# A hybrid decoder layer with 32 experts: routing and first dispatch in another order, and each pair's dispatch inside the pair before

## Chip, cores and metric

One Trainium2 chip, one of its cores. The metric is the time of one execution on the device in microseconds (us), median of the runs.

## What is computed

A decoder layer in float32 over 256 tokens of 1024 channels. First a mixer (differential attention, a pooling branch, attention into a memory, gates, output projection) gives `h`. Then a sparse layer of 32 experts, in which each token goes to its four best:

```python
logits = rmsnorm(h, g_ffn) @ w_router + b_router       # 256 x 32
top_val, top_idx = lax.top_k(logits, 4); gates = softmax(top_val)
# for every expert e, over the tokens that chose it:
g = minimum(xb @ w_gate[e] + b_gate[e], 7.0)
u = clip(xb @ w_up[e] + b_up[e], -7.0, 7.0)
out = (g * sigmoid(1.702 * g) * (u + 1.0)) @ w_down[e] + b_down[e]
y = y.at[rows].add(out * gates)                         # result: h + y
```

Each expert's three matrices are 1024 x 1024, 12.6 MB together, 403 MB for all.

## The kernel before

The code writes the program of every engine by hand: each engine runs its own list in order, with semaphores between them. There is no planner.

**The mixer** runs in 48 units of 128 tokens by 512 columns. A unit is the work of `unit_k` (line 1331 holds the products, three for each of 8 blocks), in one of three banks of PSUM. Units 44 to 47 are the output projection: columns 0 to 511 of tile 0 and of tile 1, then the other columns of both. `add_h` (L1137) adds each to the residual X, which gives h.

**Routing.** `turn_h` transposes h in four pieces (L1295), `copy_hT` (L1143) copies them with the gain to HNT, `logits` (L1541) multiplies by the router's weights. ScalarE sums the squares of h (`h_square`, L789), GpSimd (POOL) makes the inverse root of the mean (L483, L485, `inverse_root`). On VectorE `route` (L1160 to L1174) scales the logits, takes the four best and writes MASK; `weigh` (L1181 to L1184) makes the gates; `norm_h` (L1151) writes the normalised rows HN. When both tiles have a mask, TensorE multiplies them by a triangular matrix and by ones (L1561). That gives each token's rank in each expert and each expert's number of tokens, from which VectorE computes the number of rounds (each has room for SLOTS = 64 tokens per expert; here one round is enough). L1565 transposes the gates; L1570 reads the number of rounds into a register of TensorE.

**The experts** run in 16 pairs. `build_slots` compares iota with the ranks: PT (L1227), 128 tokens by 2 x 64 slots in 0 and 1, and PW (L1224), the same times the gates. At the start of a pair TensorE dispatches (L1612): HN by PT gives the gathered rows XE, transposed, in banks 4 and 5, which ScalarE (L808) and VectorE (L1255) copy. L1617 transposes PW. Then `project` (L1592, with the biases at L1598 and L1599) for gate and up of the first expert, `combine` (L1580) adds the pair before into the tokens, `project` for the second expert, and for each expert the transposes of its activations AH (L1295), a copy by ScalarE (L819) and the product with w_down (L1644), copied by L822 and L1280. `slots_free` says that PW is transposed; then VectorE builds the slots of the next pair and BIAS_PICK (L1259), before it reads bank 0 (L1263, signal `g_read`).

**The weights.** Each pair needs twelve loads of 2 MB, in the order gate, gate, up, up of the first expert, the same of the second, then w_down twice for each. They go to nine slots of 16 KB a partition (`experts_ring`). SP issues them in order (L415); a load waits until the slot's last load has been used (semaphore `used`, once for each load). Eighteen loads of a turn of 24 run over the nine slots twice, the last six take only six of them:

```python
MOE_SLOT = (8, 5, 4, 6, 0, 2, 1, 3, 7)
TURN_SLOT = [MOE_SLOT[q % RING] for q in range(2 * RING)] + [MOE_SLOT[q] for q in range(1, 7)]
```

So in the second pair, load 27 (counted from 0) takes the slot of load 20, load 28 that of 21. The first nine loads are issued while the mixer ends, gated by its units; the last of these waits for both logits.

## Time and profile before

| | |
|---|---|
| time, median of 3 runs | 1244.7 us (1244.56 to 1244.71) |
| the profiled execution | 1244.2 us, its span 1242.2 us |
| mean granted clock of TensorE | 0.996 |
| TensorE busy | 1166.5 us (94%), weight loads 578.7 us |
| VectorE, ScalarE, GpSimd busy | 440.4, 259.1, 49.3 us |
| moved by DMA | 458.51 MB, mean 369 GB/s |
| chain that ended last | PE 75%, DMA 17%, DVE 4%, ACT 2%, issue 2% |

PE is TensorE, DVE VectorE, ACT ScalarE, POOL GpSimd, SP the engine that issues the loads. L with a number is a line of the kernel. The page cuts the span into 40 slices. The chain that ended last is followed back from the last instruction, at each step to what released it. A pair of numbers at the start of a row is start and duration in us. Matmuls in float32 are run in two passes, so a count (x32) is twice the number of products in the code; passes are pipelined, and the mean of one overlaps the next.

### The profile page before, as it was taken

To read this page: it belongs to the slowest core of one execution; us is meant where nothing else is said; L and a number is where in the kernel's file an instruction comes from. 1 tells how busy PE (TensorE), PEld (TensorE's weight loads), DVE (VectorE), ACT (ScalarE), POOL (GpSimd) and SP (SyncE) were. 2 spreads that over 40 slices of the span, in tenths; PEclk is the share of its full clock that TensorE was granted. 3 is DMA by queue.
4 is the path that set the end of the run, shared out by engine and by line. 5 is a ranking of instruction groups with operands and counts; after the bars stand their busy time and mean duration, and the time that the engine had idled before them with its cause. 6 is when DMAs were issued, how large, how long until landed. Compare 5 with 4: busy or idle time off the path is not lost.

```text
span 1242.2 us, 13980 instructions
## 1 busy us (share of the span) xinstructions
PE 1166.5 (94%) x5428; PEld 578.7 (47%) x5428; DVE 440.4 (35%) x775; ACT 259.1 (21%) x414; POOL 49.3 (4%) x72
## 2 busy tenths in 40 slices
PE   8999999998899999999999999999999999999897
PEld 5887888877434434343434344343434332433332
DVE  4878798765412121212122122212122121212122
ACT  5555477531100100010001001000100010010100
POOL 2222101101000000000000000000000000000000
PEclk9999999999899999999999999999999999999999
DMA  9455545597799999999999999999999999999996
GB/s 361 153 195 169 194 147 202 185 348 304 309 425 394 394 430 429 428 428 429 429 428 428 428 430 428 427 428 429 429 428 427 429 429 428 427 429 429 428 428 271
DMA packets 54825, 458.51 MB, mean 369 GB/s; under 512 B 4304, under 2 KB 5200, under 8 KB 30224
## 3 DMA queue, kind: packets, MB, share of 16 engines
q1 hardware_dynamic: 53408, 454.15, 88.4%
q0 software_dynamic: 1104, 3.93, 0.9%
q8 instruction: 15, 0.25, 0.1%
q10 hardware_dynamic: 288, 0.10, 0.0%
q14 instruction: 10, 0.08, 0.0%
HBM read 457.11 MB, written 1.05 MB: 369 GB/s over the span
## 4 chain that ended last, share of the span: by engine, by line
PE 75%; DMA 17%; DVE 4%; ACT 2%; issue 2%; POOL 0%; SPq 0%; POOLq 0%; DVEq 0%
PE bank L1592 30%; PE bank L1331 15%; DMA experts_ring<-in_w_down 15%; PE bank L1644 14%; PE bank L1612 5%; PE bank L1580 4%; PE bank L1598 2%; DMA ring<-in_w_mem_kv 1%; ACT region L819 1%; PE bank L1295 1%; PE bank L1599 1%; DMA ring<-in_w_out 1%; DVE ring_split L839 1%; DVE region L1246 1%; ACT region L822 1%
## 5 line engine op out<-in xcount | busy, mean ns | idle before, releaser
L1592 PE MATMUL bank<-experts_ring,region 128*64 128x512 f32 x2048 | 454.2, 596 | 11.5 <-DVE region L1255 6.5
L1592 PEld LDWEIGHTS bank<-experts_ring,region 128*64 128x64 f32 x2048 | 145.1, 137 | 291.9 <-issue 286.4
L1644 PE MATMUL bank<-experts_ring,region 128*64 128x512 f32 x1024 | 229.0, 596 | 32.0 <-ACT region L819 25.0
L1331 PE MATMUL bank<-ring_split,region_split 128*128 128x512 f32 x736 | 217.0, 396 | 0.5 <-DVE ring_split L850 0.3
L1644 PEld LDWEIGHTS bank<-experts_ring,region 128*64 128x64 f32 x1024 | 73.1, 137 | 167.3 <-issue 125.7
L1331 PEld LDWEIGHTS bank<-ring_split,region_split 128*128 128x128 f32 x736 | 136.0, 188 | 31.1 <-issue 2.3
L839 DVE TENSOR_TENSOR ring_split<-ring,ring_split 128x2048 fp32r<-128x2048 f32 x42 | 96.2, 2291 | 41.4 <-ACT ring_split L588 41.1
L1331 PE MATMUL bank<-ring_split 128*128 128x512 f32 x272 | 106.4, 391 | 0.0
L1280 DVE COPY region<-bank 64x512 f32<-64x512 f32 x32 | 22.2, 693 | 237.3 <-PE bank L1644 237.3
L1263 DVE TENSOR_SCALAR region<-bank 128x512 f32<-128x512 f32 x32 | 22.1, 692 | 209.7 <-PE bank L1599 209.7
L588 ACT ACTIVATE ring_split<-ring 128x2048 fp32r<-128x2048 f32 x42 | 80.3, 1912 | 30.8 <-DMA ring<-in_w_in 10.0
L1270 DVE TENSOR_SCALAR region<-bank 128x512 f32<-128x512 f32 x32 | 22.1, 692 | 180.0 <-PE bank L1599 180.0
L812 ACT ACTIVATE region<-region 128x512 f32<-128x512 f32 x32 | 20.2, 630 | 287.6 <-DVE region L1263 287.6
L1580 PE MATMUL bank<-region 128*128 128x512 f32 x136 | 65.7, 606 | 13.4 <-DVE region L1246 12.4
L822 ACT ACTIVATE region<-bank 64x512 f32<-64x512 f32 x32 | 18.9, 590 | 242.1 <-PE bank L1644 242.1
L1612 PEld LDWEIGHTS bank<-region 128*128 128x128 f32 x512 | 60.1, 197 | 15.3 <-issue 12.2
L1612 PE MATMUL bank<-region 128*128 128x128 f32 x512 | 63.1, 283 | 2.6 <-DVE region L1224 2.6
L1331 PEld LDWEIGHTS bank<-ring_split 128*128 128x128 f32 x272 | 51.1, 188 | 11.1
L1246 DVE TENSOR_TENSOR region<-bank,region 128x512 f32<-128x512 f32 x68 | 45.4, 687 | 14.3 <-PE bank L1580 14.3
L1580 PEld LDWEIGHTS bank<-region 128*128 128x128 f32 x136 | 24.2, 189 | 46.2 <-DVE region L1246 31.7
L1295 PE MATMUL bank<-con,region 128*128 128x128 f32 x240 | 37.0, 286 | 7.0 <-DMA con<-in_table 4.6
L816 ACT ACTIVATE region<-bank 128x256 f32<-128x256 f32 x16 | 6.1, 383 | 173.3 <-PE bank L1580 173.3
(163 smaller groups left out, 677.4 us busy)
## 6 DMA issues: line engine op xcount, KB each, us to landing
experts_ring<-in_w_gate SPq DMA_DIRECT2D x64, 2048.0 KB, 26.1
experts_ring<-in_w_up SPq DMA_DIRECT2D x64, 2048.0 KB, 25.2
experts_ring<-in_w_down SPq DMA_DIRECT2D x64, 2048.0 KB, 28.0
ring<-in_w_in SPq DMA_DIRECT2D x28, 1024.0 KB, 5.2
ring<-in_w_mem_kv SPq DMA_DIRECT2D x4, 1024.0 KB, 11.4
ring<-in_w_b_attn SPq DMA_DIRECT2D x4, 1024.0 KB, 6.3
ring<-in_w_out SPq DMA_DIRECT2D x4, 1024.0 KB, 8.7
region<-in_b_gates POOLq DMA_DIRECT2D x6, 512.0 KB, 4.5
```

Of the source, the lines that this page charges most:

```text
L588: nc.scalar.activation(upper(H), raw(H), ACT.Copy).then_inc(hi_act, 1)
L822: nc.scalar.activation(OE[e * SLOTS:(e + 1) * SLOTS, 0:HALF], bank[2][0:SLOTS, :], ACT.Copy).then_inc(o_lo, 1)
L839: nc.vector.tensor_tensor(lower(H), raw(H), upper(H), ALU.subtract).then_inc(lo_ready, 1)
L1246: nc.vector.tensor_tensor(X[:, t, h * HALF:(h + 1) * HALF], bank[6 + j % 2][:, :], X[:, t, h * HALF:(h + 1) * HALF], ALU.add).then_inc(y_a ...
L1280: nc.vector.tensor_copy(OE[e * SLOTS:(e + 1) * SLOTS, HALF:D], bank[2][SLOTS:2 * SLOTS, :]).then_inc(o_hi, 1)
L1295: ins = nc.tensor.transpose(dst[:, b * P:(b + 1) * P], srcs[b], ident)
L1331: ins = nc.tensor.matmul(UB[u % 3][:, :], a[:, k, toks], b[:, cols], start=(k == 0 and m == 0), stop=(k == k_n - 1 and m == 2))
L1580: nc.tensor.matmul(bank[6 + j % 2][:, :], PWT[:, t * P:(t + 1) * P], OE[:, h * HALF:(h + 1) * HALF], start=True, stop=True).then_inc(comb_ ...
L1592: ins = nc.tensor.matmul(dst[h * SLOTS:(h + 1) * SLOTS, :], XE[:, kk, e * SLOTS:(e + 1) * SLOTS], w[:, k, h * HALF:(h + 1) * HALF], start= ...
L1598: nc.tensor.matmul(dst[:, :], pick, BIAS_UP, start=False, stop=False)
L1612: ins = nc.tensor.matmul(bank[4 + half][:, b * P:(b + 1) * P], HN[:, t, 4 * half + b, :], PT[:, t, :], start=(t == 0), stop=(t == NT - 1))
L1644: ins = nc.tensor.matmul(bank[2][h * SLOTS:(h + 1) * SLOTS, :], AHT[:, k, half * SLOTS:(half + 1) * SLOTS], w[:, k, h * HALF:(h + 1) * HAL ...
```

## The change

- TensorE's order around units 46 and 47: tile 0's first transposes stand inside unit 46, two more inside unit 47, tile 0's logits and half of tile 1's before the last three blocks of unit 47. Tile 0's rank products come right after unit 47, its dispatch after tile 1's logits; tile 1 adds its part to both. Tile 1's logits go to bank 0.
- `norm_h` is gone. `gain_h` writes HN as h times the gain, in four halves; the inverse root is multiplied into PT instead. `route` has one operation less, and the last square covers half of tile 1's row, since the other half's is taken earlier (POOL adds the two).
- iota counts from 1, so that the ranks need no subtraction.
- The first pair's dispatch and the copies of XE stand before the loop. In the loop the dispatch of the next pair stands behind the transposes of the first expert's activations, also in the last pair. PW's transposes stand behind the first `project`.
- HN moves to another buffer and keeps its columns in order; w_gate and w_up are laid out to match on the host, by `projection_rows`.

```diff
-    c[:, C_IOTA:C_IOTA + P] = np.tile(np.arange(SLOTS), 2)[None, :]
+    c[:, C_IOTA:C_IOTA + P] = np.tile(np.arange(SLOTS) + 1, 2)[None, :]
...
+def projection_rows(w):
+    w = np.asarray(w)
+    return np.ascontiguousarray(w.reshape(EXPERTS, KD, P, D).transpose(0, 2, 1, 3).reshape(EXPERTS, D, D))
...
 # gpsimd
-            for t in range(NT):
-                pool.wait_ge(squares, 5 + t)
-                inverse_root(stat[:, 4 + t:5 + t], EPS, h_inv)
+            pool.wait_ge(squares, 6)
+            inverse_root(stat[:, 4:5], EPS, h_inv)
+            pool.wait_ge(squares, 7)
+            inverse_root(stat[:, 5:6], EPS, h_inv, stat[:, 6:7])
...
 # scalar
+            def xe_lower_half(n):
+                act.wait_ge(disp_done, n * 2 + 1)
+                nc.scalar.activation(XE[:, 0:4, :], bank[4][:, :].rearrange("p (k n) -> p k n", k=4),
+                                     ACT.Copy).then_inc(xe_lo, 1)
+            h_square(0, X[:, 1, 0:HALF], 5, 2)
+            h_square(1, X[:, 0, :], 4, 3)
+            logit_exp(0)
+            h_square(2, X[:, 1, HALF:D], 6, 4)
+            logit_exp(1)
+            xe_lower_half(0)
...
-                        act.wait_ge(disp_done, it * 2 + 1)
-                        nc.scalar.activation(XE[:, 0:4, :], bank[4][:, :].rearrange("p (k n) -> p k n", k=4),
-                                             ACT.Copy).then_inc(xe_lo, 1)
...
                             nc.scalar.activation(AHT, bank[3][:, :].rearrange("p (j s) -> p j s", j=4),
                                                  ACT.Copy).then_inc(actT_copied, 1)
+                            if e == 0:
+                                xe_lower_half(it + 1)
...
 # vector
-            def norm_h(t):
+            def gain_h(t, h):
+                cols = slice(h * HALF, (h + 1) * HALF)
                 dve.wait_ge(late_in, 32)
...
+                nc.vector.tensor_tensor(HN[:, t, cols], X[:, t, cols], GFF[:, cols], ALU.mult).then_inc(hn_ready, 1)
...
-                nc.vector.memset(zero, 0.0)
...
+                link(nc.vector.tensor_tensor_scan(run, equal, no_logits, count, ALU.add, ALU.add))
+                link(nc.vector.scalar_tensor_tensor(out=equal, in0=run, scalar=float(TOP_K), in1=equal, op0=ALU.is_le, op1=ALU.mult))
...
+            add_h(44)
+            gain_h(0, 0)
+            add_h(45)
+            copy_hT(0, 0, 0)
+            gain_h(1, 0)
+            add_h(46)
+            copy_hT(1, 1, 0)
+            copy_hT(2, 0, 1)
+            gain_h(0, 1)
             route(0)
             weigh(0)
             add_h(47)
...
+            def expert_slots(first, t):
+                for e in range(2):
+                    cols = slice(e * SLOTS, (e + 1) * SLOTS)
+                    nc.vector.tensor_scalar(PT[:, t, cols], iota[:, cols], RANKS[:, t, bass.ds(first + e, 1)],
+                                            stat[:, 4 + t:5 + t], ALU.is_equal, ALU.mult).then_inc(slots_built, 1)
...
+            dve.wait_ge(first_rank_done, 1)
+            dve.wait_ge(mask_ready, 1)
+            first_slots(0, bank[3][:, 0:32])
             copy_hT(3, 1, 1)
-            norm_h(0)
             route(1)
-            weigh(1)
-            norm_h(1)
-            dve.wait_ge(gate_ready, 2)
+            gain_h(1, 1)
             dve.wait_ge(rank_done, 1)
+            dve.wait_ge(mask_ready, 2)
+            first_slots(1, bank[3][:, 32:64])
...
+            weigh(1)
+            dve.wait_ge(gate_ready, 2)
+            xe_upper_half(0)
+            expert_weights(0)
+            next_round_pair(slice(0, NT))
...
-                        dve.wait_ge(disp_done, it * 2 + 2)
-                        nc.vector.tensor_copy(XE[:, 4:8, :], bank[5][:, :].rearrange("p (k n) -> p k n", k=4)).then_inc(xe_hi, 1)
-                        dve.wait_ge(slots_free, it + 1)
-                        build_slots(i * 2 + 2)
...
+                        dve.wait_ge(slots_free, it + 1)
+                        for t in range(NT):
+                            expert_slots(i * 2 + 2, t)
+                        expert_weights(i * 2 + 2)
...
+                        xe_upper_half(it + 1)
...
 # tensor
-            unit(46)
...
+            unit_k(46, 0, 4)
+            pe.wait_ge(h_ready, 1)
+            turn_h(0, 0, 0)
+            unit_k(46, 4, KD)
             unit_k(47, 0, 2)
+            pe.wait_ge(h_ready, 3)
+            turn_h(1, 1, 0)
+            turn_h(2, 0, 1)
+            unit_k(47, 2, 5)
             pe.wait_ge(hT_copied, 3)
             pe.wait_ge(late_in, 32)
-            logits(0)
-            unit_k(47, 2, KD)
+            logits(0, 0, KD)
+            logits(1, 0, 4)
+            unit_k(47, 5, KD)
+            pe.wait_ge(mask_ready, 1)
+            nc.tensor.matmul(bank[3][:, 0:32], tri, MASK[:, 0, :], start=True, stop=True)
...
             pe.wait_ge(h_ready, 4)
             turn_h(3, 1, 1)
             pe.wait_ge(hT_copied, 4)
-            logits(1)
+            logits(1, 4, KD)
+            pe.wait_ge(slots_built, 2)
+            pe.wait_ge(hn_ready, 3)
+            dispatch_tile(0)
             pe.wait_ge(mask_ready, 2)
...
+            pe.wait_ge(slots_built, 4)
+            pe.wait_ge(hn_ready, 4)
+            dispatch_tile(1)
             pe.wait_ge(gate_ready, 2)
...
-                        pe.wait_ge(slots_built, it * 8 + 4)
-                        for half in range(2):
-                            for b in range(4):
-                                for t in range(NT):
-                                    ins = nc.tensor.matmul(bank[4 + half][:, b * P:(b + 1) * P], HN[:, t, 4 * half + b, :], PT[:, t, :],
-                                                           start=(t == 0), stop=(t == NT - 1))
-                            ins.then_inc(disp_done, 1)
+                        pe.wait_ge(xe_lo, it + 1)
+                        pe.wait_ge(xe_hi, it + 1)
+                        project(it, turn, s, 0, 0, 0, bank[0])
                         pe.wait_ge(slots_built, it * 8 + 8)
                         for t in range(NT):
                             ins = nc.tensor.transpose(bank[3][:, t * P:(t + 1) * P], PW[:, t, :], ident)
                         ins.then_inc(slots_free, 1)
-                        pe.wait_ge(xe_lo, it + 1)
-                        pe.wait_ge(xe_hi, it + 1)
-                        project(it, turn, s, 0, 0, 0, bank[0])
                         project(it, turn, s, 0, 1, 2, bank[1])
...
                             turn4(bank[3], [AH[:, e, j * P:(j + 1) * P] for j in range(4)], actT_done)
+                            if e == 0:
+                                dispatch(it + 1)
```

`dispatch_tile(t)` is tile t's eight products of a dispatch, `dispatch(n)` waits for the slots of pair n and runs both tiles. `first_slots(t)` makes RANK from the rank products and builds tile t's two columns of PT; `expert_weights` builds PW as `build_slots` did; `xe_upper_half(n)` is VectorE's copy of bank 5.

## Rows read from the trace of the kernel before

**Rows 1.** The page's forty slices: TensorE's clock in tenths, bytes per second.

```profile
PEclk9999999999899999999999999999999999999999
...
GB/s 361 153 195 169 194 147 202 185 348 304 309 425 394 394 430 429 428 428 429 429 428 428 428 430 428 427 428 429 429 428 427 429 429 428 427 429 429 428 428 271
```

**Rows 2.** Table by stretches: length, busy by engine, granted clock, DMA share, GB/s.

```profile
308.00:318.20 10.20, 6.35 (x29) 5.88 (x30) 6.77 (x35) 1.79 (x3) 0.00 (x0) 0.50 0.99 423
320.00:326.00 6.00, 5.18 (x28) 1.87 (x28) 2.57 (x10) 0.29 (x1) 0.00 (x0) 1.00 0.01 3
326.00:380.00 54.00, 51.05 (x241) 19.98 (x239) 12.86 (x24) 4.60 (x8) 0.00 (x0) 1.00 1.00 415
380.00:427.00 47.00, 44.66 (x196) 15.87 (x194) 9.61 (x13) 3.42 (x6) 0.00 (x0) 1.00 0.95 383
427.00:1225.00 798.00, 749.93 (x3482) 292.25 (x3478) 179.88 (x336) 81.81 (x126) 0.00 (x0) 1.00 1.01 429
```

**Rows 3.** Timeline of TensorE, 287 to 337 us, with idle time before.

```profile
296.42 1.88 PE L1541 MATMUL bank<-region 128*128 128x32 f32 x16
...
303.26 0.66 PE L1295 MATMUL bank<-con,region 128*128 128x128 f32 x4 [0.79 <-DVE region L1137]
304.70 1.97 PE L1541 MATMUL bank<-region 128*128 128x32 f32 x16 [0.78 <-DVE region L1143]
309.22 2.34 PE L1561 MATMUL bank<-region,con 128*128 128x32 f32 x10 [2.55 <-DVE region L1174]
...
321.18 7.09 PE L1592 MATMUL bank<-experts_ring,region 128*64 128x512 f32 x32 [0.82 <-DVE region L1255]
```

**Rows 4.** The chain that ended last, 300 to 430 us: start, duration, what.

```profile
302.51 0.70 DVE region L1137
...
307.11 0.26 DVE region L1160
...
314.62 5.54 PE bank L1612 x32
...
373.21 3.77 PE bank L1612 x32
...
377.81 7.09 PE bank L1592 x32
...
413.55 0.60 ACT region L819
...
414.20 7.11 PE bank L1644 x32
...
422.76 7.09 PE bank L1644 x32
```

**Rows 5.** The loads' line, 417 to 419 us: load 27, issue and landing.

```profile
L415 SPq DMA_DIRECT2D experts_ring<-in_w_up x1: 333/333/333, 417.9 to 417.9; - x1
...
DMA to landing us min/median/max: 9.3/9.3/9.3
```

**Rows 6.** Timeline of POOL, 295 to 308 us: both inverse roots' powers.

```profile
296.07 0.58 POOL L485 TENSOR_TENSOR stat<-stat,small 128x1 f32<-128x1 f32 x1
...
304.78 2.30 POOL L485 TENSOR_TENSOR stat<-stat,small 128x1 f32<-128x1 f32 x1
```

**Rows 7.** The tile `rounds`: TensorE's load of the number of rounds, with its start.

```profile
L1570 PEldq TENSOR_LOAD <-rounds x1: 488/488/488, 313.3 to 313.3; - x1
```

**Rows 8.** The loads' line, 409 to 410 us: landing of load 25.

```profile
DMA to landing us min/median/max: 7.3/7.3/7.3
```

**Rows 9.** The loads' line, 412 to 414 us: landing of load 26.

```profile
DMA to landing us min/median/max: 9.2/9.2/9.2
```

**Rows 10.** Timeline of TensorE, 1214 to 1236 us: the last pair's w_down products.

```profile
1215.04 0.60 PE L1295 MATMUL bank<-con,region 128*128 128x128 f32 x4
...
1225.79 3.65 PE L1644 MATMUL bank<-experts_ring,region 128*64 128x512 f32 x16 [0.88 <-ACT region L819]
1230.43 3.65 PE L1644 MATMUL bank<-experts_ring,region 128*64 128x512 f32 x16 [0.99 <-DMA experts_ring<-in_w_down]
```

More of the change, by code:

```diff
@@ L1284, in _ @@
                 dve.wait_ge(rank_ready, r * 2 + 3)
-                next_round_pair()
+                next_round_pair(slice(0, NT))
                 dve.wait_ge(rank_ready, r * 2 + 4)
@@ L1533, in _, with logits @@
             unit(45)
-            unit(46)
             def turn_h(n, t, h):
                 turn4(bank[3 + n], [X[:, t, (4 * h + b) * P:(4 * h + b + 1) * P] for b in range(4)], hT_done)
-            def logits(t):
-                for k in range(KD):
-                    ins = nc.tensor.matmul(bank[7][:, t * EXPERTS:(t + 1) * EXPERTS], HNT[:, k, t * P:(t + 1) * P], WR[:, k, :],
+            def logits(t, first, after):
+                for k in range(first, after):
+                    ins = nc.tensor.matmul(bank[(7, 0)[t]][:, 0:EXPERTS], HNT[:, k, t * P:(t + 1) * P], WR[:, k, :],
@@ L1542, in logits, with dispatch_tile @@
                                            start=(k == 0), stop=(k == KD - 1))
-                ins.then_inc(logit_done, 1)
-            for n, (t, h) in enumerate(((0, 0), (1, 0), (0, 1))):
-                pe.wait_ge(h_ready, n + 1)
-                turn_h(n, t, h)
+                if after == KD:
+                    ins.then_inc(logit_done, 1)
+            def dispatch_tile(t):
+                for half in range(2):
+                    for b in range(4):
+                        ins = nc.tensor.matmul(bank[4 + half][:, b * P:(b + 1) * P], HN[:, t, (4 * half + b) * P:(4 * half + b + 1) * P],
+                                               PT[:, t, :], start=(t == 0 and b == 0), stop=(t == NT - 1), skip_group_check=True)
+                    if t == NT - 1:
+                        ins.then_inc(disp_done, 1)
```

100 lines of the change are left out of this document (48 added, 52 removed).

## Prediction

> **What bounds the kernel now.** I read the slices of the page first, to see which resource is full in which part. TensorE's clock is full nearly everywhere, and from the sixteenth slice on the bytes per second stand at 427 to 430 GB/s without a dip [rows 1]. The expert stage streams 192 loads of 2048 KB, which is 2.097 MB each; at 429 GB/s one takes 4.89 us and the twelve of a pair of experts 58.7 us. The table by stretches then shows where this stream is not full: nothing moves between 320 and 326 us, only 383 GB/s between 380 and 427, and 429 from there to 1225 [rows 2]. In the chain that ended last, a pair takes TensorE 56.63 us (321.18 to 377.81) [rows 3, 4]. So TensorE is 2 us a pair quicker than the stream: while it still has the ring of slots full, loads wait for slots that TensorE frees; once that lead is used up, only the stream counts. The end of the kernel is therefore the landing of the load that was last held up for a slot, plus 4.89 us for each load behind it, plus a tail. I count loads from 0. Every step of 4.89 us from load 27 on is of that unbroken kind, so load 27, issued at 417.9 and landed 9.3 us later [rows 5], fixes the rest. It takes the slot of load 20, the first w_down load of the second pair. Because SP issues in order and slots come back in the order of the turn, it waits for that load to be used.
>
> So a gain on the way to the first pair reaches the end only as far as it frees the slot of load 20 earlier. That is where I work it out: start of the first pair, length of that pair, place of load 20 in the next, landing, tail.
>
> **The start of the first pair.** Before, it is 321.18 [rows 3]. I walk the new order with the durations of the old one, at the full clock.
> - Unit 46 ends with four transposes inside it instead of behind, unit 47 with half of the second logits inside. The transposes are only moved. Half the logits is half of 1.88 us, 0.94 [rows 3]. Unit 47, which ended at 302.5 (the residual add that reads it starts at 302.51 [rows 4]), ends at 303.45. That delays the residual add, and SP's loads 6 and 7, by 0.95 us. Nobody needs those before 334 us.
> - The first tile's routing runs on VectorE from about 300.6, behind both its logits and the copy work, and takes 2.0 us; it ends before unit 47 and TensorE does not wait for it. Its three rank products, six of the logits' 0.12 us passes (0.7 us), fill the time in which TensorE waited for the residual add, which was 0.79 us idle [rows 3].
> - Add 303.5 to 304.2, transposes to 304.9, copy to 305.65 (0.7 each as before), half the logits 0.95 to 306.65. While TensorE transposes, VectorE builds the first tile's ranks and slots (0.25 and twice 0.25), which the copy just waits out.
> - Before, the second route waited for the inverse root: POOL's power took 2.30 us beside VectorE's long normalisation, against 0.58 alone [rows 6], and the route began at 307.11 [rows 4]. Now the last square is over half a row, the long normalisation is gone and the gains are applied elsewhere. So root ready at 306.3, route at 306.8. It ends at 308.75 with one operation less (2.1 us before, from 307.11 [rows 4] to the ranks at 309.22 [rows 3]).
> - TensorE does the first tile's dispatch (half of 3.77 us, 1.9 [rows 4]) from 306.65 to 308.6, covered by that route. Without that cover it would cost its 1.9 us. Then four rank passes (0.5) to 309.3; gain_h(1,1), 0.7 us, runs beside them and just covers them.
> - Ranks and slots of the second tile 0.8 us to 310.2, dispatch 1.9 to 312.1, copies of XE 0.7 to 312.8. The gate weights, the count of rounds and the weighted slots (2.7 us before the old dispatch) lie beside or behind this on VectorE. TensorE's transposes of the gates and its load of the round count follow the dispatch; from that load at 313.3 to the first work behind it at 314.62 were 1.3 us [rows 4, 7], the same as would give 313.4 to 313.7 here.
> By rows 313.8. A dozen hand-overs are each rounded to 0.05 us, and I take 314.2, bounds 313.7 and 315.5: **7.0 us earlier**. Part of it is the clock: the old stretch 308 to 318.2 ran at half of it (1.2 GHz) [rows 2], and the dispatch in it took 5.54 us instead of 3.77 [rows 4].
>
> **The pair.** The dispatch no longer stands between two pairs. From its start to the next project were 4.6 us (373.21 to 377.81, [rows 4]); what is left is a restart, for which no row stands (bounds 0 and 0.6, the issue gap there; I take 0.25). The two transposes of PW go behind the first projection and still cost about 0.4. The dispatch goes behind the transposes of AH, 3.77 us; it hides the wait for ScalarE's copy, 0.67 us (413.53 to 414.20 [rows 4]). Sum −4.6 + 0.25 + 0.4 + 3.77 − 0.67 = **−0.9 us a pair**. But load 20 is the first behind that dispatch: within its pair it is used 0.4 + 3.1 = **3.5 us later**. The slots of the next pair (1.7 us on VectorE) are now built only after PW's transposes, ahead of the read of bank 0. That delays g_read by about 2 us, but TensorE needs that bank only after the next projection and the combine, 8 us or more on, so nothing. BIAS_PICK is built at the start of the pair and first read 7 us on, the halves of XE are copied some 15 us before their first product: nothing either.
>
> **Landing.** Load 27 is issued 7.0 + 0.9 − 3.5 = 4.4 us earlier (bounds 2.9 and 4.9). The stream in front of it no longer reaches so far: loads 25 and 26 are issued over 7 us earlier and land by about 414, just when load 27 is issued. A load that found the stream nearly empty landed in 7.3 us [rows 8], against the 9.3 of load 27 [rows 5], but the one behind it lost about 1 us (load 26 took 9.2 [rows 9]). I give load 27's train 8.7 us, 0.6 better than before; bounds 0 and 1.4. The unbroken stream, and so the end of it at 1230.4, comes **5.0 us earlier**.
>
> **Tail.** In the last pair a dispatch is done too, for a pair that doesn't exist. Before, TensorE was still ahead of the stream: it took the third w_down load at 1225.79, was done with it 0.99 us too early for the last, and took that at 1230.43 [rows 10]. Now the first w_down product starts after a dispatch, at about 1219.3 in the old time, runs through two loads (7.1), and with the 8.56 us between the starts of two such products (414.20 to 422.76 [rows 4]) the last two begin at 1227.85 and end at 1234.95 instead of 1234.1: **+0.9**, bounds 0.6 and 1.4. All loads have the same size and the packets of w_gate and w_up stay as long; their new order costs the device nothing.
>
> Sum: −5.0 + 0.9 = **−4.1 us**. The profiled execution took 1244.2 (span 1242.2) and would take 1240.1; the median of the runs, 1244.7, becomes **1240.6**. In short, the change is the start of the first pair minus 318.3: every us of that start counts in full.
>
> **The rivals.**
> - The clock falls again. Before, it fell at 308.0 after TensorE had done only logits of 32 columns, 2.0 us of work in the 4.1 us before [rows 2, 3]. In the new order transposes and a dispatch stand in that place, which speaks against; waits remain between 303.5 and 306.7, which speaks for. The price is 1.8 us for a whole dispatch and about 0.1 us for each rank, logits or transpose pass, together 2 us: start at 316.2, time **1242.6**. The Trainium skill (TensorE: Matmul & The Clock Gate, The HAM clock gate) says that the throttled clock is the default and recent activity releases it; by that rule thinning out dense work, as here in front of the ranks, speaks for this rival.
> - The ring doesn't hold. If the queue in front of load 27 were still over 4 us long, the delay of 3.5 us inside the pair would not be felt, and the end would be earlier by 7.0 + 0.9 − 0.9 or so: **1237.7**. Against it: that load already had just enough queue before.
> - The stream is the bound anyway, and the some 13 us of gaps in it (6.0, 1.8 and 5.0 us by the bytes of three stretches [rows 2]) don't depend on TensorE's start (loads 6 to 8 even come 0.95 us later). Then only the tail is left: **1245.6**. Against it: the gap from 320 to 326 ends with the first used slot.
> - Slower: the mid-pair dispatch holds load 20's slot while the routing gives nothing back, because a half clock through the whole of it (44 passes more at 0.1 us) and a slow root (1.7 us) eat the 7.0. Start 321.2, 3.5 − 0.9 − 0.6 + 0.9 = +2.9: **1247.6**. It would be slower from a start at 320.8 on. No row shows both at once.
>
> **How the numbers follow.** A measurement of this kernel can tell about 0.2%, 2.5 us, from no change. Forecast 0.62, of its own 1239.2 to 1242.2 (start 313.7 to 315.5, the bounds of landing and tail half used); clock 0.18; ring free 0.07; stream alone 0.07; slower 0.06. Faster by over 2.5 us means under 1242.2: forecast and free ring, 0.69. Within: 0.25. Slower, 0.06. The range from 1238.6 to 1244.0 takes in the forecast and the clock, 0.80.
>
> **What would show it.** The first expert product starts near 314; no stretch of half clock, or one of few us; the power on POOL takes 0.6 us; the first pair lasts 55.7; load 27 is issued near 413.5 and lands 8 to 9 us later; no gap in the stream behind it; the last two loads are multiplied without a wait between them. It would be wrong if the start lies after 316, if another load than 27 is the last one held, or if TensorE's restart between the pairs is longer than 1 us.

## The result, and the profile after

The changed kernel takes **1238.55 us** (median of 5 runs, 1237.13 to 1239.02) against 1244.7 before: ratio 0.9947, 95% interval 0.9936 to 0.9959. That is 6.15 us less; 4.1 were forecast, and the time lies 0.05 us under the lower end of the range. The same kernel run again (after_again below) took 1237.43. The profiled execution took 1238.0 with a span of 1236.2 us.

The page's slices after: TensorE's clock in tenths and bytes per second. Against [rows 1] the slice of 8 tenths is gone, and the dip that followed the start of the loads takes one slice (297) instead of two (304 and 309).

```profile
PEclk9999999999999999999999999999999999999999
...
GB/s 360 153 199 170 189 153 204 177 342 297 412 388 429 397 429 428 428 428 428 428 429 428 429 428 429 428 429 428 429 427 429 428 429 428 430 427 430 427 430 253
```

The table by stretches after, to be read beside [rows 2] (stretch, length, busy time by engine, granted clock, DMA share, GB/s):

```profile
302.00:306.00 4.00, 3.02 (x23) 2.54 (x22) 2.59 (x8) 0.72 (x2) 0.87 (x2) 0.99 0.62 193
306.00:309.30 3.30, 3.30 (x17) 3.30 (x17) 2.35 (x10) 0.32 (x1) 0.00 (x0) 0.50 0.96 412
309.30:314.00 4.70, 2.84 (x24) 2.43 (x22) 3.24 (x17) 0.97 (x2) 0.00 (x0) 1.00 1.03 439
320.00:326.00 6.00, 6.00 (x30) 2.22 (x28) 3.11 (x10) 0.63 (x1) 0.00 (x0) 1.00 0.96 393
326.00:380.00 54.00, 52.36 (x250) 20.65 (x246) 12.63 (x24) 4.33 (x8) 0.00 (x0) 1.00 0.97 406
380.00:427.00 47.00, 45.34 (x216) 18.69 (x214) 10.71 (x15) 5.52 (x9) 0.00 (x0) 1.00 0.99 407
427.00:1218.00 791.00, 739.30 (x3444) 289.48 (x3442) 184.06 (x333) 70.34 (x115) 0.00 (x0) 1.00 1.01 428
```

The stretch from 320 to 326, which carried 3 GB/s before, now carries 393 GB/s; 380 to 427 rose from 383 to 407. The half clock (0.50, the lower of the two levels, 1.2 GHz) is left in one stretch of 3.3 us instead of 10.2.

TensorE's timeline after, from the ranks of the first tile to the first expert product (start, duration, what, idle time before it and who ended it), beside [rows 3]:

```profile
302.54 0.30 PE L1609 MATMUL bank<-region,con 128*128 128x32 f32 x2
...
303.49 0.66 PE L1331 MATMUL bank<-con,region 128*128 128x128 f32 x4 [0.20 <-DVE region L1155]
304.93 1.08 PE L1576 MATMUL bank<-region 128*128 128x32 f32 x8 [0.78 <-DVE region L1161]
305.84 3.66 PE L1584 MATMUL bank<-region 128*128 128x128 f32 x16
309.34 0.31 PE L1621 MATMUL bank<-region,con 128*128 128x32 f32 x2
...
310.72 2.05 PE L1584 MATMUL bank<-region 128*128 128x128 f32 x16 [0.85 <-DVE region L1226]
...
314.04 4.51 PE L1656 MATMUL bank<-experts_ring,region 128*64 128x512 f32 x20 [1.05 <-DVE region L1239]
```

The start of the first pair came from 321.18 to 314.04. The same 16 passes of a dispatch take 3.66 us in the half clock and 2.05 out of it.

The seams of the pair, first in the kernel before (last w_down products, dispatch, gate transposes, next projection; then transposes of AH and the w_down products), then after (transposes, dispatch, w_down; then last w_down and next projection):

```profile
366.12 7.09 PE L1644 MATMUL bank<-experts_ring,region 128*64 128x512 f32 x32 [0.87 <-ACT region L819]
373.14 3.84 PE L1612 MATMUL bank<-region 128*128 128x128 f32 x32
376.81 0.38 PE L1617 MATMUL bank<-con,region 128*128 128x128 f32 x2
377.81 7.09 PE L1592 MATMUL bank<-experts_ring,region 128*64 128x512 f32 x32 [0.61 <-issue]
...
412.92 0.60 PE L1295 MATMUL bank<-con,region 128*128 128x128 f32 x4
414.20 2.37 PE L1644 MATMUL bank<-experts_ring,region 128*64 128x512 f32 x10 [0.69 <-ACT region L819]
```

```profile
349.35 0.60 PE L1331 MATMUL bank<-con,region 128*128 128x128 f32 x4
349.78 3.74 PE L1584 MATMUL bank<-region 128*128 128x128 f32 x32
353.45 7.09 PE L1703 MATMUL bank<-experts_ring,region 128*64 128x512 f32 x32
...
361.99 7.09 PE L1703 MATMUL bank<-experts_ring,region 128*64 128x512 f32 x32 [0.87 <-ACT region L835]
368.91 3.61 PE L1656 MATMUL bank<-experts_ring,region 128*64 128x512 f32 x16
```

From the start of the last w_down products to the next projection: 11.69 us before (366.12 to 377.81), 6.92 after (361.99 to 368.91), 4.77 less. From the transposes of AH to w_down: 1.28 before (412.92 to 414.20), 4.10 after (349.35 to 353.45), 2.82 more. The first pair lasts 54.87 us instead of 56.63.

In the loads' own records load 27 is issued at 411.98 and lands 7.36 us later, load 28 is issued at 415.56 and lands 9.94 us later:

```profile
L423 SPq DMA_DIRECT2D experts_ring<-in_w_up x1: 333/333/333, 412.0 to 412.0; - x1
...
DMA to landing us min/median/max: 7.4/7.4/7.4
```

```profile
L423 SPq DMA_DIRECT2D experts_ring<-in_w_gate x1: 332/332/332, 415.6 to 415.6; - x1
...
DMA to landing us min/median/max: 9.9/9.9/9.9
```

A landing is reported in sixteen parts, and these times are those of the last part. By the last parts load 27 comes 5.63 us behind load 26 and load 28 comes 6.16 behind load 27; by the mean of the parts it is 6.03 and 4.99. Behind them the steps are 4.89 to 4.98 by the mean. POOL's power now takes 0.57 us, against the 2.30 of [rows 6]:

```profile
304.68 0.57 POOL L493 TENSOR_TENSOR stat<-stat,small 128x1 f32<-128x1 f32 x1
```

The last pair after, to be read beside [rows 10]: a dispatch for nobody, and then two w_down loads at a time without a wait between them.

```profile
1209.95 2.51 PE L1584 MATMUL bank<-region 128*128 128x128 f32 x21
1212.39 7.09 PE L1703 MATMUL bank<-experts_ring,region 128*64 128x512 f32 x32
1219.41 0.66 PE L1331 MATMUL bank<-con,region 128*128 128x128 f32 x4
1220.95 7.09 PE L1703 MATMUL bank<-experts_ring,region 128*64 128x512 f32 x32 [0.88 <-ACT region L835]
```

### The profile page after: what moved, and what is told of

Its sections match the earlier page's. It is cut to its first block, busy times and chain, and to the rows that moved or that the text cites. A ratio compares the mean times of both kernels' runs of the same rounds, so it can differ in the third digit from the quotient of the medians.

```text
span 1236.2 us, 14082 instructions
## 1 busy us (share of the span) xinstructions
PE 1165.1 (94%) x5460; PEld 581.9 (47%) x5460; DVE 446.3 (36%) x775; ACT 249.8 (20%) x409; POOL 47.8 (4%) x72
## 4 chain that ended last, share of the span: by engine, by line
PE 67%; DMA 28%; DVE 3%; ACT 1%; issue 1%; SPq 0%; POOL 0%; DVEq 0%; POOLq 0%
PE bank L1656 26%; DMA experts_ring<-in_w_up 26%; PE bank L1367 17%; PE bank L1703 8%; PE bank L1644 5%; PE bank L1584 4%; PE bank L1662 2%; PE bank L1331 1%; DMA ring<-in_w_mem_kv 1%; DVE region L1281 1%; PE bank L1663 1%; DMA ring<-in_w_out 1%; DVE ring_split L857 1%; ACT ring_split L597 0%; PE bank L1576 0%
## 5 line engine op out<-in xcount | busy, mean ns | idle before, releaser
L1584 PEld LDWEIGHTS bank<-region 128*128 128x128 f32 x544 | 63.8, 196 | 1.0 <-DVE region L1226 1.0
L1226 DVE TENSOR_SCALAR region<-con,region,stat 128x64 f32<-128x64 f32 x68 | 16.8, 310 | 124.9 <-PE bank L1677 124.9
L1644 PEld LDWEIGHTS bank<-region 128*128 128x128 f32 x136 | 24.1, 188 | 46.2 <-DVE region L1281 31.7
```

The source lines that it names most:

```text
L1584: ins = nc.tensor.matmul(bank[4 + half][:, b * P:(b + 1) * P], HN[:, t, (4 * half + b) * P:(4 * half + b + 1) * P], PT[:, t, :], start=(t ...
L1644: nc.tensor.matmul(bank[6 + j % 2][:, :], PWT[:, t * P:(t + 1) * P], OE[:, h * HALF:(h + 1) * HALF], start=True, stop=True).then_inc(comb_ ...
```

## The experiments

My theory after the comparison: the end of the stream follows the start of the first pair one for one; the new loop as such is worth nothing to the stream and costs 0.9 us in the tail. The rivals: the loop order gives part of the gain (the prediction's −0.9 a pair), or the stream takes up part of a later start.

One reading carries all that follows. A load reports its landing in sixteen parts. The product can start only with the sixteenth, but that one comes by chance 0.3 to 2.5 us behind the mean of them, so I compare the **mean landing of the last load** with the start (the first product of the first pair). "Mixer to start" runs from the start of TensorE's last product of the mixer to that start, and "to the end" from the last part of the last landing to the profiled time, which is 1.8 to 2.0 us more than the span. For all profiled executions, in us:

| kernel | mixer to start | start | mean landing | difference | last part behind mean | to the end | profiled time | median |
|---|---|---|---|---|---|---|---|---|
| before | 19.31 | 321.17 | 1229.10 | 907.93 | 1.29 | 13.81 | 1244.2 | 1244.7 |
| after | 11.95 | 314.04 | 1221.94 | 907.91 | 1.44 | 14.61 | 1238.0 | 1238.55 |
| after_again | 10.85 | 313.85 | 1221.74 | 907.89 | 1.09 | 14.60 | 1237.43 | 1237.43 |
| loop_only | 19.96 | 322.06 | 1229.94 | 907.88 | 1.19 | 14.77 | 1245.9 | 1245.92 |
| start_late | 14.26 | 316.55 | 1224.36 | 907.81 | 0.31 | 14.59 | 1239.26 | 1239.59 |
| fill | 11.53 | 315.33 | 1223.22 | 907.89 | 1.33 | 14.64 | 1239.2 | 1238.42 |
| tile0_late | 14.60 | 317.37 | 1225.32 | 907.95 | 1.15 | 14.67 | 1241.14 | 1241.45 |
| dispatch_end | 11.01 | 314.40 | 1223.15 | 908.75 | 1.66 | 16.93 | 1241.74 | 1241.61 |
| short_dispatch | 11.01 | 312.85 | 1216.91 | 904.06 | 1.39 | 13.70 | 1232.0 | 1233.5 |
| ring8 | 10.84 | 313.39 | 1220.35 | 906.96 | 1.59 | 14.36 | 1236.3 | 1236.45 |
| ring8_again | 11.96 | 314.47 | 1221.56 | 907.09 | 2.54 | 14.37 | 1238.47 | 1238.47 |
| late_ring8 | 14.27 | 316.43 | 1223.39 | 906.96 | 1.03 | 14.61 | 1239.02 | 1239.98 |
| end_ring8 | 11.95 | 314.22 | 1220.86 | 906.64 | 1.20 | 16.93 | 1238.99 | 1239.6 |
| before_ring8 | 20.12 | 322.12 | 1228.84 | 906.73 | 2.30 | 13.80 | 1244.94 | 1244.01 |

The start has two parts of chance. TensorE's last product of the mixer starts anywhere from 301.85 to 303.81 us in these executions, and 0.9 us apart in two of one kernel (after and after_again); why, no run shows. And where the granted clock falls in front of the first dispatch, the way from the mixer to the start takes 11.95 us instead of 10.85 (last section).

**loop_only**: the kernel before with the new loop alone. The routing keeps its old order; the dispatch of pair 0 goes in front of the loop, that of the next pair behind the transposes of AH, the slots behind PW's transposes.

```diff
+            dispatch(0)
...
-                        pe.wait_ge(slots_built, it * 8 + 4)
-                        for half in range(2):
...
+                            if e == 0:
+                                dispatch(it + 1)
```

> The kernel before with the loop of the change alone: dispatch behind the first transposes of AH, PW's transposes behind the first projection, the first dispatch ahead of the loop; routing, normalisation and host layout as before. Both theories: the start stays near 321.2, pair 54.9. Theory A: load 20 is used 3.0 later in its pair and the pair is 1.8 shorter, so load 27 becomes the last held one and the stream ends 0.2 to 0.6 us later than before; tail +0.9. Time 1246.0, so the loop's part of the change is a loss of 1.3. Theory B: 1245.7, tail alone. If the in-loop move were a gain (shorter pairs reach the end), it would be 1243 or less.

Measured 1245.92 us (ratio 1.0008, 0.9999 to 1.0017). The medians alone don't tell this from no change; the traces do. The difference from start to landing is 907.88 against 907.93: the loop alone moves the stream by 0.05 us, and costs about 1 us at the end (14.77 against 13.81). The start is 0.9 us later than in the profiled execution of before, and so it is in before_ring8, which has the old loop: in both the clock fell before the logits were done (3.33 and 3.38 us for the passes that took 1.97 in [rows 3]), so this isn't the loop's doing.

**dispatch_end**: the changed kernel with the dispatch and both copies of XE behind the pair's last product.

```diff
-                            if e == 0:
-                                dispatch(it + 1)
...
+                        dispatch(it + 1)
```

> The changed kernel with the next pair's dispatch and its two copies of XE moved behind the last product of the pair, as in the kernel before; the routing stays new. Theory A (the end is set by the last load that waits for its slot): first product at 314.0, pair 56.8 us instead of 54.9, w_down of the second pair used 3 us earlier in its pair. Loads 27 and 28 are no longer the last ones held; loads 25 and 26 are, issued near 402.3 and 406.4. The stream behind ends where that of the changed kernel does (near 1223.5), and the extra dispatch behind the very last product costs 2.7 us of tail instead of 0.9. Time 1240.3, 1.7 above the changed kernel. Theory B (only the start of the first pair and the tail count, the ring does not): the same start, so the same sum, 1240.3. Both agree in the total here, and the trace separates them by which load is the last with a step over 4.9 us.

Measured 1241.61 us (ratio 0.9974, 0.9964 to 0.9984), 1.3 over what was expected. The chain of its end shows the extra dispatch of the expectation: in the last pair the dispatch for nobody stands between the last product and the combine.

```profile
1225.94 2.57 PE bank L1700 x12
1228.51 3.77 PE bank L1583 x32
1232.28 1.73 PE bank L1643 x4
```

The kernel before did no dispatch there: from the last part's landing to the end are 16.93 us here and 13.81 before, 3.1 more where 2.7 were expected. So this kernel isn't a clean undoing of the loop's part, its time says nothing for the new loop, and loop_only has to decide. Its stream lies 0.84 us behind that of after, and 0.82 behind that of before. Loads 25 and 26 were held here, as in before (7.06 and 5.73 us behind the one in front by the mean, against 6.97 and 5.27). Half of the 0.82 can be read: load 25 is issued 88.41 us behind the start instead of 87.99, as the transposes of PW now stand inside the pair ahead of the use that frees its slot, and the first pair takes 56.82 us instead of 56.63. The other half stays open.

**start_late**: 32 passes of 128 columns, used by nobody (DELAY is 16), on TensorE ahead of the dispatch of the second 128 tokens.

```diff
+            for n in range(DELAY):
+                nc.tensor.matmul(bank[1][:, (n % 4) * P:(n % 4 + 1) * P], HN[:, 0, 0:P], PT[:, 0, :], start=True, stop=True)
```

> The changed kernel with 16 products (32 passes) more on TensorE ahead of the second tile's dispatch, into an unused bank: the start of the first pair is 3.75 us later and nothing else changes. Theory A and B: every us of the start counts in full, 1238.55 + 3.75 = 1242.3. Rival (the stream is the bound anyway): 1238.6. A value between, about 1240.5, would say that half of a delay is taken up by queued loads.

Measured 1239.59 us (ratio 0.9966, 0.9952 to 0.9979), 1.0 later than after where 3.7 were expected. By the total that looks like a stream that takes up a later start. It isn't: the clock stayed full in its routing, so that the way from the mixer to the start is 2.3 us longer than in after (3.4 longer than in after_again, where the clock was full too) and the start only 2.5 later. The mean landing followed by 2.42, and the last part came 0.31 us behind the mean instead of 1.44.

**tile0_late**: the dispatch of the first 128 tokens back behind the ranks and slots of the second.

```diff
-            pe.wait_ge(slots_built, 2)
-            pe.wait_ge(hn_ready, 3)
-            dispatch_tile(0)
...
             pe.wait_ge(hn_ready, 4)
+            dispatch_tile(0)
             dispatch_tile(1)
```

> The changed kernel with the dispatch of the first 128 tokens moved back behind the ranks and slots of the second, directly in front of its own dispatch: this part of the change undone alone. Theory A, in the changed kernel that dispatch (2.03 us) fills a wait of TensorE for the ranks of the second tile (2.25 us from the end of the logits to 309.05 with 0.26 us of wait left) and costs the path nothing; moved back it stands on it: start 2.05 us later, 315.4 to 316.1, last load landing (mean) 907.9 behind the start, 1239.5 to 1240.5 us. Theory B, the empty wait in its place also lets the clock fall, as in the kernel before: both dispatches at half of it, start near 318.5 to 319.5, 1243 us.

Measured 1241.45 us (ratio 0.9976, 0.9966 to 0.9986): between the two. Table by stretches and TensorE's timeline of this kernel:

```profile
307.00:309.30 2.30, 0.48 (x3) 0.48 (x3) 2.09 (x10) 0.32 (x1) 0.00 (x0) 0.54 1.01 435
309.30:311.00 1.70, 0.84 (x4) 0.71 (x5) 1.07 (x8) 0.00 (x0) 0.00 (x0) 0.50 1.06 453
311.00:314.00 3.00, 3.00 (x15) 3.00 (x16) 1.11 (x8) 0.00 (x0) 0.00 (x0) 0.50 1.01 431
```

```profile
308.82 0.64 PE L1618 MATMUL bank<-region,con 128*128 128x32 f32 x2 [2.13 <-DVE region L1190]
...
310.74 5.38 PE L1584 MATMUL bank<-region 128*128 128x128 f32 x32 [0.86 <-DVE region L1226]
...
317.37 3.21 PE L1654 MATMUL bank<-experts_ring,region 128*64 128x512 f32 x13 [1.04 <-DVE region L1239]
```

TensorE now waits 2.13 us, the clock is at a half from 307.2 to 314, and the 32 passes take 5.38 us where two fast halves take 4.1. From the mixer to the start are 14.60 us, 3.75 more than in after_again with its full clock: the dispatch's own 2.05 us and 1.7 of clock. After had a fall of its own there, so against it the way is 2.65 longer, and the other 0.7 of its 3.3 us earlier start is a mixer that ended earlier. The median is 2.9 us above that of after, 4.0 above that of after_again.

**fill**: one product of 512 columns in each of two waits of TensorE in front of the second half of the logits.

```diff
+            fill(1)
             pe.wait_ge(h_ready, 4)
             turn_h(3, 1, 1)
+            fill(1)
```

> The changed kernel with one product of 512 columns, used by nobody, in each of two waits of TensorE between the last work on w_out and the second half of the logits. In the profiled execution of the changed kernel the granted clock was 0.50 from 306 to 309.3, tile 0's dispatch took 3.66 us instead of 2.03 and the ranks behind it began 1.3 us after their mask. Theory A, the clock falls there in most executions because of the waits in front: with the two products it stays full, the start lies near 312.8 to 313.4 and the time is 1.0 to 1.2 us shorter, 1237.4. Theory B, the fall is seldom (it was absent in three profiled executions of kernels with the same code there): no difference, 1238.5. If the products delay what stands behind them, 1239.0.

Measured 1238.42 us (ratio 0.9953, 0.9941 to 0.9964), no difference. The start of its profiled execution is 315.33 and not 312.8 to 313.4: the mixer ended 1.7 us later than in after, and from there to the start are 11.53 us, 0.7 more than in after_again, the work that the products add. The mean granted clock of all six executions is 1.000 to three places; of the 49 executions of the nine kernels that have the change's order up to there, 28 have 1.000 and 21 less. So the products may well keep the clock up, at a price that takes back most of the 1.1 us; six executions don't show it.

**short_dispatch**: the loop's dispatch cut to two products. It leaves out the gathering of the tokens' rows for every pair behind the first; all waits stay.

```diff
-                for t in range(NT):
-                    dispatch_tile(t)
+                for half in range(2):
+                    nc.tensor.matmul(bank[4 + half][:, 0:P], HN[:, 0, 0:P], PT[:, 0, :], start=True, stop=True).then_inc(disp_done, 1)
```

> The changed kernel with the dispatch inside the loop cut to one product for each half of the slots (the tokens' rows are not gathered for the pairs behind the first, so this part of the computation is left out; every wait and every other instruction stays). Theory A, the dispatch inside the pair is what holds the stream after the change: with it from one use of a load to the next are 7.61 us (349.52 to 357.13), without it some 4.8, so the first pair lasts 52.1 instead of 54.87 and load 20 is used 5.6 us earlier; load 27 is issued at 406.3 instead of 411.98; the last held loads are then 25 and 26 (issued near 397.6 and 401.5), load 28 lands near 421.5 instead of 425.5 (mean of its parts 421.0 instead of 424.0), and the tail loses its 0.9 us: 1234.3 us, 1233.3 to 1235.7. Theory B, the stream is held by other waits and the dispatch costs only its part of the tail: load 28 lands where it did, 1237.6 us.

Measured 1233.5 us (ratio 0.9912, 0.9899 to 0.9925), 0.8 under Theory A and within its range, with a start that was 1.2 us earlier (full clock, and a mixer that ended 0.2 earlier), which the theory had not counted. The first pair's seam shrinks to

```profile
348.61 0.61 PE L1592 MATMUL bank<-region 128*128 128x128 f32 x4
349.46 7.09 PE L1703 MATMUL bank<-experts_ring,region 128*64 128x512 f32 x32 [0.24 <-ACT region L835]
```

the landing comes 3.85 us nearer to the start (904.06) and the end is 0.9 us shorter (13.70). With this order of slots the dispatch counts in the stream at its old place and at its new one alike (loop_only); being shorter helps.

**ring8**: another order of slots. In the first turn loads 9 to 11 take the slots of loads 1 to 3, load 12 that of load 0 and load 13 that of load 5; before, loads 9 to 17 each took the slot of the one nine ahead.

```diff
-TURN_SLOT = [MOE_SLOT[q % RING] for q in range(2 * RING)] + [MOE_SLOT[q] for q in range(1, 7)]
+TURN_SLOT = list(MOE_SLOT) + [5, 4, 6, 8, 2, 1, 3, 0, 5, 4, 6, 7, 2, 1, 3]
```

> The changed kernel with another map of loads to slots: six slots are reused every 8 loads and three every 12, so that no load has to wait for a load that is less than 8 places ahead of it (it was 7 at the start of each turn, among them load 27 on load 20). Theory A: load 27 now waits for load 19 (issued near 404.4 instead of 412.0) and 28 for load 20, and neither is held; in exchange load 9 waits for load 1 and is issued near 321.8 instead of 317.9, which makes one of loads 9 to 13 the last held. The unbroken stream starts there and ends 1.6 us earlier: 1237.0. Theory B (the ring does not count): 1238.6; or 1242.5, if the start of load 9, 3.9 us later, counted in full.

Measured 1236.45 us (ratio 0.9933, 0.9919 to 0.9946), 0.5 under Theory A. Theory A wanted the stream's end 1.6 us earlier than in after, and the mean landing came 1.59 earlier; but 0.65 of that is the earlier start, and 0.95 the order of slots. The stream is thinner at first and whole sooner (ring8, then after):

```profile
321.00:326.00 5.00, 5.00 (x25) 1.76 (x25) 3.17 (x10) 0.63 (x1) 0.00 (x0) 1.00 0.75 252
...
345.00:427.00 82.00, 79.46 (x391) 33.96 (x389) 17.58 (x30) 8.84 (x14) 0.00 (x0) 1.00 1.01 428
```

```profile
321.00:326.00 5.00, 5.00 (x26) 2.07 (x26) 3.11 (x10) 0.63 (x1) 0.00 (x0) 1.00 0.98 410
...
345.00:427.00 82.00, 79.47 (x390) 33.19 (x388) 17.56 (x30) 8.84 (x14) 0.00 (x0) 1.00 0.97 402
```

**late_ring8** is start_late's 32 passes with this order, **before_ring8** the kernel before with it, **end_ring8** dispatch_end with it.

> ring8 with 16 products (32 passes of 128 columns) more on TensorE ahead of the loop, as in the run named start_late; nothing of them is used. The start comes 3.4 us later (316.8). Theory A, the start counts in full: load 13 issued near 344.8, mean landing of the last load 1223.8 instead of 1220.35, 1239.9 us (1239.2 to 1240.6). Theory B, the stream takes part of a later start up in its queue, as the medians of start_late (1.0 us later for 2.5 us of start) suggest: 1237.8 us.

Measured 1239.98 us (ratio 0.9963, 0.995 to 0.9976): Theory A. Start and mean landing both move by 3.04 us against ring8, to the hundredth.

> The kernel before with the other order of slots alone (loads 9 to 12 wait for the slots of loads 1 to 4 and loads 13 to 23 for those of a later turn, as in the run named ring8). Theory A, with this order the last load that is held is 13, which waits for load 5 to be used, in the first pair and ahead of any dispatch inside the loop: then the whole stream follows the start, and between this kernel and ring8 lies the start (321.2 against 313.39, 7.8 us) less the tail (0.9): 1236.45 + 6.9 = 1243.3 us, load 13 issued near 349.2 and the last load landing near 1229.7. Theory B, in the kernel before the dispatch between the pairs still holds loads 25 and 26 in this order too: loads 25 or 26 show a step over 5.3 us and the time stays 1244.7.

Measured 1244.01 us (ratio 0.9991, 0.9982 to 0.9999), 0.7 over Theory A and 0.7 under B; the trace decides for A: load 13 is issued at 349.89, from there to load 31 no load's mean comes more than 4.99 us behind that of its forerunner, and the difference is 906.73. (The expectation has load 12 wait for the slot of load 4. It takes that of load 0, and by the order of issue waits for what load 11 waits for.)

> ring8 with the dispatch and both copies of XE behind the pair's last product again, as in the run named dispatch_end: the early routing of the change, the dispatch where it was before, the other order of slots. In the runs so far the mean landing of the last load is the start plus a constant: 906.96 for ring8 and late_ring8, 906.73 for before_ring8, 908.75 for dispatch_end. Theory A, with the other order of slots the stream depends on nothing behind load 13, so the place of the dispatch is nothing to it (constant 906.7 to 907.0) and only the tail counts, which is 0.94 us shorter with the dispatch at the pair's end: 1235.5 us, 0.9 below ring8. Theory B, the dispatch between the pairs costs the stream as much as in dispatch_end (constant 908.75 against 907.9, +0.85): 1236.4, no difference from ring8.

Measured 1239.6 us (ratio 0.9961, 0.9947 to 0.9975). On the stream Theory A holds (906.64), on the time I missed by 4 us. The expectation counts the tail as 0.94 us shorter and leaves out the dispatch for nobody behind the last product, which that of dispatch_end had counted: here too 16.93 us lie between the last part and the end, against 14.36 in ring8.

> The kernel named ring8 once more, for a comparison with end_ring8 and the changed kernel on the same chip in the same stretch of time: 1236.4 us, constant 906.96.

> The changed kernel once more. 1238.5 us (1237.1 to 1239.1). Mean landing of the last load 907.9 us behind the start; its start at 314.0 if the granted clock falls to a half near 306 again, at 313.0 to 313.4 with a full clock, which was what the other profiled kernels with this routing showed.

On another chip: ring8 1238.47 (ratio 0.995, 0.9937 to 0.9964), after 1237.43 (0.9946, 0.9932 to 0.9959). In its two profiled executions ring8's landing is 0.8 to 0.95 us nearer to the start than that of after. After_again's start was expected at 313.0 to 313.4 with a full clock, and it had that clock and 313.85: its mixer ended 0.9 us later than that of after. The rest of ring8's lead in the first comparison was luck: here its start was 1.08 us later (the clock, below) and its last part 2.54 us behind the mean. That it beats the changed kernel is not shown.

## Why the prediction was right or wrong

**Start: right, the number in part by luck.** 314.04 for 314.2. The second route starts at 306.12, 0.9 us behind the root (POOL 0.57 us), the first dispatch fills a wait, the weights of the gates are off the path. Only the early dispatch was undone in a run: tile0_late prices it at 3.75 us of the way from the mixer to the start with a full clock, 2.65 against after. That the other two give the rest is read from the trace, not tested. Two misses cancel in the number: unit 47 ended at 302.7 instead of 303.45, and the half clock came back for 3.4 us, which I had made a rival's whole case. It cost 1.1 us of the start (313.39 in ring8, 314.47 in ring8_again), not 2, as the second dispatch came after it. From the end of unit 47 to the start after_again with its full clock took 10.23 us, and the forecast by rows 10.35.

**Every us of the start counts in full: right**, and better than I could know: in the seven executions with the old order of slots and the whole dispatch (dispatch_end aside), with starts from 313.85 to 322.06, landing less start is 907.81 to 907.95.

**The loop's part in the stream: this step failed.** The prediction took load 27 for the load that fixes the end in the kernel before, and let the loop's order delay the stream by what it delays that load's slot: 3.5 less 0.9 less 0.6, so 2.0 us lost of the 7.0. loop_only shows the loop's order worth 0.05 us to the stream, and with the whole change the mean landing of the last load comes 7.16 us earlier where 5.0 were forecast. In the kernel before, load 27 was not held. It came 4.89 us behind load 26, as any load of the unbroken stream, and was issued 4.4 us before load 26 had landed (load 26 was issued at 413.11; with that [rows 5] and [rows 9] already give both figures). Held were 25 and 26, on the slots of loads 18 and 19, whose use stands ahead of the place where the dispatch now stands.

The steps behind the load in front, by the mean of the parts (loop_only has the old routing):

| load | before | after | loop_only |
|---|---|---|---|
| 25 | 6.97 | 5.37 | 5.39 |
| 26 | 5.27 | 5.41 | 5.35 |
| 27 | 4.89 | 6.03 | 6.09 |
| 28 | 4.89 | 4.99 | 4.98 |

Loads 25 and 26 are issued 8.7 us earlier after, and what they waited beyond the stream's own step falls from 2.46 us to 1.00. Load 27 becomes the last one clearly held, and it and load 28 now wait 1.24. Together that is 2.24 us instead of 2.46, and the 0.2 between them is lost again in slightly longer steps behind load 28. This is why the loop's order is worth nothing to the stream: it gives to 25 and 26 what it takes from 27. Why the two come out so nearly equal, no run shows.

In the terms of the sum, by load 27:
- Pair: forecast −0.9, measured −1.76. The removed seam was worth 4.77 us, not 4.6 less a restart of 0.25: the next projection starts with no gap at all, and the 0.61 us issue gap of before stood behind the transposes that went away with the dispatch. PW's transposes cost 0.2, not 0.4. The dispatch behind the transposes of AH costs 2.82 net, not 3.10.
- Load 20 is used 3.0 us later in its pair, not 3.5. So load 27 was issued at 411.98, 5.92 us earlier instead of 4.4: these terms, and 0.14 of the start, are 1.5 us of the miss.
- Train: forecast 0.6. Load 27 found 1.0 us of queue in front of its mean landing instead of 3.6, and its own took 7.02 us from the issue instead of 8.53: 1.5 better, outside the bounds of 0 and 1.4. (From the issue of 27 to the last part of 28 it is 14.22 against 13.52, 0.7 better; but 0.7 us more of lag of the last part is in that.) Of the 0.9 missed here 0.26 is lost behind load 27.

**Tail: right.** From the last landing to the end of the last product are 3.77 us instead of 2.82, +0.95 for +0.9; short_dispatch takes it back.

Sum by the measured terms: −7.14 for the start, nothing for the loop, +0.95 for the tail: −6.2. The two spans differ by 6.03, since the last part's lag behind the mean adds 0.15; the profiled times differ by 6.2, the medians by 6.15. The rival "the ring doesn't hold" named the nearer time, 1237.7, but by a mechanism that isn't there: the ring does hold, at other loads. The slower rival's sum doesn't close: 4.4 and 1.7 are 6.1 us and not 7.0, so it should have named 1246.7; nothing else hangs on it.

Of the named signs the start, the root, the stream without a gap and the last two loads came. Load 27 was issued at 411.98 and landed 7.4 us later, not near 413.5 and 8 to 9 later, and the first pair lasts 54.87 us, not 55.7: the signs that missed are those of the step that failed.

## What to carry to other kernels

When a ring of buffers feeds a slower stream, list the step of every load behind the one in front, by the mean of its parts, not the wait of one: those over the stream's own step are the held ones, and an edit that relieves them can hold their neighbours by as much. A load whose step is the stream's own does not yet pass on a delay of its slot in full. Work moved between two uses within a pair changes which load is held, work taken away changes the end. For small differences compare a landing's mean with the start; totals carry a microsecond of luck. And look what a moved step does in the last round of a loop.

## What was not expected of the hardware

**The sixteen parts of a landing.** The last part came 0.31 to 2.54 us behind the mean in fourteen profiled executions, and can keep that lag over the whole unbroken stream (in after 1.43 us at load 29 and 1.44 at load 191; in before 0.79 at load 29, with a jump at load 185 to 1.39 and 1.29 at load 191). The Trainium skill (DMA: Bandwidth & Descriptors, Why a DMA increments its semaphore by 16 and not by 1) says that the engines finish independently and only the full sixteen means landed; the trace agrees, and shows how far apart they finish here.

**The clock by chance.** ring8 and ring8_again are one kernel, and their TensorE is alike to 0.03 us from 280 us up to the first dispatch. From 306 to 309.3 the granted clock was full in the first execution and fell in the second (table by stretches of each):

```profile
306.00:309.30 3.30, 2.96 (x25) 2.66 (x24) 2.39 (x11) 0.32 (x1) 0.00 (x0) 1.00 1.01 432
```

```profile
306.00:309.30 3.30, 3.30 (x19) 3.30 (x19) 2.35 (x10) 0.32 (x1) 0.00 (x0) 0.58 1.02 437
```

The dispatch took 2.03 us in the one and 3.53 in the other. Of the nine profiled executions with the change's order of TensorE there, three had the fall (after, ring8_again, end_ring8). In these three the way from the mixer to the start takes 11.95 or 11.96 us, in the other four without added passes 10.84 to 11.01. In tile0_late, where TensorE waited 2.13 us more, the half clock lasted longer, some 7 us, and all nine executions have a mean granted clock of 0.996 or 0.997. The kernel before's order has its own chance: there the clock fell at 308 in before and during the logits, near 305.2, in loop_only and before_ring8. By the Trainium skill (TensorE: Matmul & The Clock Gate, The HAM clock gate) the high clock has to be earned by recent activity; with tile0_late, where TensorE stood idle for longer and all nine executions fell, that agrees. But the same stretch with either clock says that with the change's order TensorE's work alone doesn't decide it; what does, no run here shows.
